# Up products of the last feed-forward: high and low activations in one 512-column matmul, halves summed on VectorE

## What is computed

```python
def swiglu(h, wg, wu, wd):
    return (jax.nn.silu(h @ wg) * (h @ wu)) @ wd

x = x + 0.5 * m(8) * ffn(ada(x, lp['norm_ffn2'], m(6), m(7)), 'ffn2')   # D_MODEL 1024, D_FF 2816
```

## Time and profile before

| | us |
|---|---|
| median of 3 runs | 2188.58 |
| profiled execution, span from the first to the last instruction | 2186.5 |
| TensorE (PE) busy, whole span | 2146.8 (98%) |
| VectorE (DVE) busy | 1447.5 (66%) |
| ScalarE (ACT) busy | 1022.0 (47%) |
| GpSimd (POOL) busy | 616.9 (28%) |
| chain that ended last, share of PE | 90% |

### The profile page before, as it was taken

One profiled execution on the slowest core, in us unless ns is written; L12 is line 12 of the kernel. 1 busy time (PEld: TensorE's weight loads), 2 busy tenths in 40 slices (PEclk: granted clock), 3 DMA queues, 4 the chain that ended last, 5 costly groups with the idle time before them and its releaser, 6 DMA issues.

```text
span 2186.5 us, 32383 instructions
## 1 busy us (share of the span) xinstructions
PE 2146.8 (98%) x12181; PEld 1793.6 (82%) x12181; DVE 1447.5 (66%) x2042; ACT 1022.0 (47%) x1621; POOL 616.9 (28%) x615
## 2 busy tenths in 40 slices
PE   7999999999999999999999999999999999999998
PEld 4888878987766778987888898888889887889997
DVE  4887887775577456876676784445448858776555
ACT  4544445554455543553344453222235556645444
POOL 0566566402000036344444420000003201261000
PEclk9999999999999999999999999999999999999999
DMA  9476675633343354745545464444546445576564
GB/s 305 149 221 189 171 216 162 177 94 90 97 116 88 90 171 130 207 143 162 155 147 175 128 197 145 145 142 148 153 125 165 116 121 153 152 206 175 184 187 135
DMA packets 471966, 340.64 MB, mean 156 GB/s; under 512 B 13226, under 2 KB 437654, under 8 KB 471686
## 3 DMA queue, kind: packets, MB, share of 16 engines
q1 hardware_dynamic: 441312, 238.06, 37.6%
q0 software_dynamic: 29056, 96.35, 15.1%
q10 hardware_dynamic: 1446, 4.19, 0.5%
HBM read 326.96 MB, written 12.36 MB: 155 GB/s over the span
## 4 chain that ended last, share of the span: by engine, by line
PE 90%; DVE 5%; ACT 2%; issue 2%; DMA 1%; POOL 0%; SPq 0%; DVEq 0%; ACTq 0%; POOLq 0%
PE bank L832 20%; PE bank L833 20%; PE bank L837 19%; PE bank L900 4%; PE bank L910 4%; PE bank L901 3%; PE bank L984 2%; PE bank L990 2%; PE bank L985 2%; DVE w_lo L801 1%; PE bank L1358 1%; PE bank L1334 1%; PE bank L1125 1%; PE bank L1132 1%; PE bank L1126 1%
## 5 line engine op out<-in xcount | busy, mean ns | idle before, releaser
L801 DVE TENSOR_TENSOR w_lo<-raw,w_hi 128x1024 fp32r<-128x1024 f32 (+1 forms) x442 | 583.5, 1322 | 527.3 <-PE bank L837 312.6
L791 ACT ACTIVATE w_hi<-raw 128x1024 fp32r<-128x1024 f32 (+1 forms) x442 | 461.7, 1045 | 621.3 <-PE bank L833 289.2
L832 PE MATMUL bank<-h_hi,w_hi 128*128 128x512 f32 (+1 forms) x1728 | 601.5, 360 | 2.7 <-DVE X L2047 1.5
L833 PE MATMUL bank<-h_lo,w_hi 128*128 128x512 f32 (+1 forms) x1728 | 592.5, 355 | 0.0
L832 PEld LDWEIGHTS bank<-h_hi,w_hi 128*128 128x128 f32 x1728 | 326.5, 189 | 58.9 <-issue 11.8
L837 PE MATMUL bank<-h_hi,w_lo 128*128 128x512 f32 (+1 forms) x1728 | 367.1, 355 | 0.0
L833 PEld LDWEIGHTS bank<-h_lo,w_hi 128*128 128x128 f32 x1728 | 326.7, 189 | 45.4 <-issue 1.0
L837 PEld LDWEIGHTS bank<-h_hi,w_lo 128*128 128x128 f32 x1728 | 291.5, 189 | 45.5
L832 PE MATMUL bank<-inner_hi,w_hi 128*128 128x256 f32 (+1 forms) x654 | 206.2, 337 | 0.0
L833 PE MATMUL bank<-inner_lo,w_hi 128*128 128x256 f32 (+1 forms) x654 | 203.3, 332 | 0.0
L2470 POOL DMA_DIRECT2D wm<-in_w_mod_dram x128 | 92.6, 724 | 362.0 <-DVE gstage L2031 159.3
(11 more groups left out here) (305 smaller groups left out, 3483.3 us busy)
## 6 DMA issues: line engine op xcount, KB each, us to landing
wm<-in_w_mod_dram POOLq DMA_DIRECT2D x128, 512.0 KB, 4.0
raw<-in_w_in_dram SPq DMA_DIRECT2D x108, 512.0 KB, 3.9
raw<-in_ffn_w_down_dram SPq DMA_DIRECT2D x94, 512.0 KB, 3.9
raw<-in_ffn_w_gate_dram SPq DMA_DIRECT2D x88, 512.0 KB, 4.1
raw<-in_ffn_w_up_dram SPq DMA_DIRECT2D x88, 512.0 KB, 4.0
raw<-in_w_out_dram SPq DMA_DIRECT2D x24, 512.0 KB, 4.1
raw<-in_ffn_w_down_dram SPq DMA_DIRECT2D x24, 384.0 KB, 3.9
raw<-in_w_branch_dram SPq DMA_DIRECT2D x16, 512.0 KB, 4.6
```

The costliest lines, as they stand in the source:

```text
L791: act.activation(w_hi[w_slot[n]][:, 0:unit.rows, :], raw[unit.slot][:, 0:unit.rows, :], ACT.Copy).then_inc(hi_made, 1)
L801: dve.tensor_tensor(w_lo[w_slot[n]][:, 0:unit.rows, :], raw[unit.slot][:, 0:unit.rows, :], w_hi[w_slot[n]][:, 0:unit.rows, :].bitcast(F32) ...
L832: pe.matmul(psum, w_hi[s][:, k, :], hi, start=(k == 0), stop=False)
L833: mm = pe.matmul(psum, w_hi[s][:, k, :], lo, start=False, stop=False)
```

## The change

One unit of the up stages of the last feed-forward runs 8 matmuls of 512 columns and 8 of 256, in place of 24 of 256. The moving operand of the wide matmul is `h_hi` and `h_lo` of one slice side by side, so that the left half of the bank gathers the products with the high activations and the right half those with the low ones. VectorE sums the two halves by a `reduce_sum` over pairs into `wa` (gate products) or `wb` (up products). Silu then reads `wa` and the multiplication reads `wb`, both after a wait for this sum. The first four units are left as they were: 40 of the 44 up units of this feed-forward change, 20 chunks. `h_hi` and `h_lo` become the halves of one tile.

```diff
-        h_hi = sb("h_hi", [P, DC, TOK], F32R)
-        h_lo = sb("h_lo", [P, DC, TOK], F32R)
+        h_pair = sb("h_pair", [P, 2, DC, TOK], F32R)
+        h_hi, h_lo = h_pair[:, 0], h_pair[:, 1]
...
+        joined = signal("joined")
...
+        def packed_up(l, ffn):
+            return tokens(l, "ffn2") == LAT and (l, ffn) == (LAYERS - 1, 2)
...
+            def side_by_side(u, psum):
+
+                unit = units[u]
+                s = w_slot[unit.product]
+                pe.wait_ge(hi_made, unit.product + 1)
+                for k in range(DC):
+                    mm = pe.matmul(psum, w_hi[s][:, k, :], h_pair[:, :, k, 0:LAT], start=(k == 0), stop=False)
+                mm.then_inc(hi_used, 1)
+                pe.wait_ge(lo_made, unit.product + 1)
+                for k in range(DC):
+                    mm = pe.matmul(psum[:, 0:LAT], w_lo[s][:, k, :], h_hi[:, k, 0:LAT], start=False, stop=(k == DC - 1))
+                mm.then_inc(unit_done, 1)
...
-                        product(*at(u0, j, i), bank[j][:, 0:n], DC, h_rhs(n))
+                        if packed_up(l, ffn):
+                            side_by_side(u0 + 4 * i + j, bank[j][:, :])
+                        else:
+                            product(*at(u0, j, i), bank[j][:, 0:n], DC, h_rhs(n))
...
                         if j % 2 == 0:
-                            act.wait_ge(unit_done, u0 + j + 1 + i * 4)
+                            source = bank[j][:, 0:n]
+                            if packed_up(l, ffn) and (part, i) != (0, 0):
+                                joined.wait(act, (l, part, 4 * i + j))
+                                source = wa[:, (j // 2) % 2, 0:n]
+                            else:
+                                act.wait_ge(unit_done, u0 + j + 1 + i * 4)
...
-                            act.activation(wa[:, (j // 2) % 2, 0:n], bank[j][:, 0:n], ACT.Silu).then_inc(silu_done, 1)
+                            act.activation(wa[:, (j // 2) % 2, 0:n], source, ACT.Silu).then_inc(silu_done, 1)
...
                         split_lo(dve, w_next[n0 + 4 * i + j])
+                        beside = packed_up(l, ffn) and (part, i) != (0, 0)
+                        if beside:
+                            dve.wait_ge(unit_done, u0 + j + 1 + i * 4)
+                            if j % 2 == 1 and c + 2 * i >= 2:
+                                dve.wait_ge(inner_lo_made, i * 2 + (c - 1))
+                            sum_to = (wa, wb)[j % 2][:, b, 0:n]
+                            joined.done(dve.reduce_sum(sum_to, bank[j][:, :].rearrange("p (s c) -> p c s", s=2), AX_X), (l, part, 4 * i + j))
...
-                            dve.tensor_tensor(wb[:, b, cols], bank[j][:, cols], wa[:, b, cols], ALU.mult).then_inc(inner_made, 1)
+                            if beside:
+                                joined.wait(dve, (l, part, 4 * i + j))
+                            dve.tensor_tensor(wb[:, b, cols], wb[:, b, cols] if beside else bank[j][:, cols], wa[:, b, cols],
+                                              ALU.mult).then_inc(inner_made, 1)
```

## The result

The changed kernel takes 2214.18 us (median of 4 runs, 2213.74 to 2215.02) against 2188.61 for the kernel before (4 runs, 2187.95 to 2189.61): a ratio of 1.0117 with a 95% interval of 1.0103 to 1.0132, 25.6 us slower. Forecast were 2211.0, in a range from 2198 to 2224.

The account below looks back on a forecast made before the run. PE bounded the kernel before; after the change a ring through the ACT and DVE queues, 7.0 us a chunk against PE's 5.55, would. Delays of 8.0, 5.2 and 9.2, together 22.4 us, give 2211.0 us, range 2198 to 2224.

Parts of the forecast that it names:

- The bound: Last feed-forward before the change: PE busy without a break, one wait of 0.2 us, ACT and DVE with slack.
- The price of the matmuls: Changed up units on PE: 0.227 us per wide matmul, 0.12 per narrow, 2.77 a unit; 4.2 us saved over 40 units.
- the rival of the slow stream: Up units: eight wide matmuls with a two-piece operand cost more than 1.81 us; hidden up to 0.7 a unit; 1% beyond.
- The ring: Up stages: in-order ACT and DVE queues wait on each other in a closed circle, 7.0 us a chunk against PE's 5.55.
- The sum: DVE's new reduction in the up stages: 0.69 us each, 40 sums, bounds 0.42 and 0.96.
- lower bound: DVE's reduction at 0.42 us if it went by results; dropped because tensor_reduce has only the single-rate mode.
- The account by stages: Third down unit's start in the three parts of the last feed-forward: 8.0, 5.2 and 9.2 us later, together 22.4.
- The signs: Trace after: PE idle before wide matmuls from each stage's third changed chunk, two sizes by turns, waits near 22 plus 4 us.
- The clock: Last feed-forward: gaps under 1 us keep granted clock 1.00; rival of a fall to 1.2 GHz, up to 2295 us, 2%.
- the rival by the price of the sum: 40 sums in the rings: each 0.27 us is 10.8; 2200 us at 0.42, 2222 at 0.96; 4% for beyond.
- expected gain: PE's shorter up units: the whole 4.2 us comes, 2184.4 us, if the ring doesn't close above 5.55; 5%.

Follow-up runs that it names:

- TensorE's part alone: Changed kernel with the wide matmuls only: no sums, silu and multiplication read the left half of the bank, old order; 2184.81 us against 2188.74 for the kernel before.
- the first experiment: Changed kernel with, on VectorE alone, each unit's sum moved ahead of the low split of the unit two ahead; 2185.22 us against 2188.44 for the kernel before.
- silu later: Changed kernel with, on ScalarE alone, the silu moved behind the high split of the next, odd unit; 2186.00 us against 2188.74 for the kernel before.
- The halved sum: Changed kernel with the reduction reading only the left half of the bank, 256 elements for 256 results; 2202.72 us, 11.5 less than the changed kernel.
- The filled gap: Changed kernel plus four float32 matmuls of 256 columns between the second and third unit of the last down stage; 2212.71 us against 2214.18.

## Why the prediction was right, and by how much it missed

**The bound.** PE without a break and one wait of 0.2 us: right, and the kernel with TensorE's part alone shows it, since 0.1 us off each unit came off the time.

**The price of the matmuls.** Forecast 2.77 us a unit, measured 2.79; forecast gain 4.2 us, measured 3.9 where it can show. The operand in two pieces costs almost like one in one piece: where PE doesn't wait, the eight wide matmuls take 1.83 to 1.85 us, against 1.81 forecast. That is also all that is left of the rival of the slow stream.

**The ring.** Forecast with each of its links, 7.0 us; measured 7.08. That both queues are in order is what closes it: the first experiment and the one with silu later change nothing but an order and open it. The Trainium skill (TensorE: Matmul & The Clock Gate, Architectural detail: the array is 16× 32×32, on the engine queues) says that ScalarE and VectorE are strictly first in, first out; the timelines agree, DVE sitting idle for 1.43 us before a split with the next sum already due (its unit had ended on PE about 2027.9, the idle time begins at 2030.4). One sentence beside it was wrong and cost nothing: before the change the ring held not one high split but two and the silu, since all three stand in ACT's queue, so about 4.3 us and not 3.0. Both are under the 5.76 us that PE then took for two units.

**The sum.** Forecast 0.69 by the row with the same reading, measured 0.684. The halved sum shows that this row, and not the one with fewer elements, was the right one. The prediction had let its lower bound fall by the mode of the reduction alone. That was a loose step, since the mode doesn't say whether elements or results count.

**The account by stages.** Forecast 8.0, 5.2 and 9.2 us; measured 8.3, 5.6 and 9.8. The three together are 1.4 us over, and the term that was mis-sized is one link of the ring: the multiplication waits for a sum of its own engine. I took 0.03 us for the signal, as between two engines; the multiplication starts 0.13 after the sum's end (2033.01 plus 0.68, 2033.82). With the other links a little short, the ring is 0.08 longer, 1.6 us over 20 chunks at most. A small error went the other way: PE starts 0.14 us after its high weights (2030.79 plus 1.04, 2031.97), not 0.2; the 0.2 was read from an idle bracket.

**The signs.** PE's waits were forecast at 22 plus 4 us; the list says 19.5, and 28.0 with the 0.25 us that each bracket leaves out, which is the figure to compare. The gaps were forecast at about 0.4 and 0.9 us, where the prediction's own links give 0.5 and 1.0; counted in full they are 0.47 and 1.03. The first wait comes in the third changed chunk, as forecast, only in the first part (2013.60); in the other two it comes in the fourth (2084.13 and 2141.05).

**The clock.** The forecast held it at 1.00 because it looked at the ring's two gaps only. The same text had worked out that the table load delays the last down stage's third unit by 1.5 us, and did not add this to the gap there: 0.8 plus 1.5 is 2.3, close to the 2.79 us gap before this feed-forward, which had shown a lower clock. That rival was priced for the whole feed-forward, up to 107 us, and not for the one place where it could happen, where it costs 1.5. The filled gap shows this directly. The sum held no term for it; the mechanism of the forecast was right, and this is its one omission that shows in the time. The longer ring and this unit are 2.9 of the 3.2 us between 2211.0 and 2214.2; the rest is within the scatter of the runs.

**The rivals.** No gain came through, as the ring binds; the rival by the price of the sum was right about its weight: 0.27 us less for each sum gave 10.5 us between the profiled executions and 11.5 between the medians, where it said 10.8.

**Where the expected gain went.** It is not lost. The kernel with the narrow matmuls and the sums takes the same 2214 us, with 3.2 us less of waiting in the up stages.

## What to carry to other kernels

Before one adds a wait from one in-order queue to another, follow the ring: what stands ahead of the releasing instruction on its queue, what that waits for, and whether it leads back; then sum the links, since busy shares (here about 60% on VectorE and 40% on ScalarE) don't show it. Work that releases another engine belongs ahead of work with slack, here the sum ahead of the split two units early; the same 40 sums cost 29 us more in one order than in the other. A delay that adds to another in one place should be added up before one says what the clock will do.

## What the runs showed of the hardware

- A reduction out of a bank costs by what it reads, not by its results: 684 ns for 256 results from 512 elements (pairs that lie 256 apart), 418 ns for 256 results from 256 elements, 689 ns for one result from 512.
- A wait on a sum of the same engine delays the next VectorE instruction by 0.13 us from the sum's end; from VectorE to ScalarE it is 0.03 (2029.74 plus 0.69, 2030.46). Without a wait the next instruction starts before the sum's end: with silu later, a split starts 0.60 us after the start of a sum of 0.68.
- After a gap of 2.27 us, in a stretch with shorter gaps, a unit of 2.79 us took 4.31 with a granted clock of 0.58 in part, and after one of 2.01 us it took 4.45 with 0.50; with four float32 matmuls inside the gap the clock stayed at 1.00. Gaps of 0.2 to 1.3 us left it at 1.00.
- A wait of PE costs about 0.25 us more than the idle time that its row shows: 0.16 of overlap that is lost and 0.09 in a slower start (1.93 us for the first eight matmuls, against 1.84).
